# Low parts of the second recurrence's weight tiles: made by GpSimd instead of VectorE

## What is computed

```python
h = rms_norm_2(x, attn_norm)
z = h @ w_in                                   # 1024 pool, 3 x 1024 r/k/v, 288 low-rank columns
pool_out = einsum(causal_multiscale_pool(z_pool), pool_w) * pool_scale
rwkv_out = rwkv7_time_mix(...)                 # S = S*w + (S a) b' + v k', y = S r, 16 heads of 64
x = x + concat(pool_out, rwkv_out) @ w_out
x = x + square(relu(rms_norm_2(x) @ w_ffn_up)) @ w_ffn_down
x = x + sigmoid(rms_norm_2(x) @ w_ple_gate) * (p @ w_ple_proj)
```

## Time and profile before

| | |
|---|---|
| median of 3 runs | 2878.07 us (2876.27 to 2879.27) |
| the profiled execution, its own time | 2877.43 us |
| its span in the profile | 2875.6 us |
| PE busy | 2797.9 us, 97% of the span |
| DVE busy | 1897.8 us, 66% |
| ACT busy | 1493.3 us, 52% |
| POOL busy | 161.3 us, 6% |
| low parts on DVE | 901 instructions, 1119.4 us |

### The profile page before, as it was taken

One profiled execution on the slowest core, in us unless ns is written; L12 is line 12 of the kernel. 1 busy time (PEld: TensorE's weight loads), 2 busy tenths in 40 slices (PEclk: granted clock), 3 DMA queues, 4 the chain that ended last, 5 costly groups with the idle time before them and its releaser, 6 DMA issues.

```text
span 2875.6 us, 40645 instructions
## 1 busy us (share of the span) xinstructions
PE 2797.9 (97%) x16324; PEld 2445.5 (85%) x16324; DVE 1897.8 (66%) x2237; ACT 1493.3 (52%) x2026; POOL 161.3 (6%) x131
## 2 busy tenths in 40 slices
PE   8999999999999999999999998989999999999998
PEld 8988987888888888888888997877788888888886
DVE  6467765555668777777777676666666666666665
ACT  5346555544455545455546565545544444444464
POOL 1010111000000000000000022111000000000000
PEclk9999999999999999999999999999999999999999
DMA  6544443466666666666665532222555565555554
GB/s 221 186 154 145 153 123 114 136 196 187 184 195 185 194 191 195 190 189 187 190 192 177 187 125 69 94 74 92 177 190 191 186 196 192 187 196 191 192 169 161
DMA packets 133820, 485.47 MB, mean 169 GB/s; under 512 B 14944, under 2 KB 16352, under 8 KB 133120
## 3 DMA queue, kind: packets, MB, share of 16 engines
q1 hardware_dynamic: 133632, 482.87, 53.1%
HBM read 480.71 MB, written 2.10 MB: 168 GB/s over the span
## 4 chain that ended last, share of the span: by engine, by line
PE 84%; DVE 7%; ACT 4%; issue 3%; DMA 1%; POOL 0%; DVEq 0%; ACTq 0%; SPq 0%; POOLq 0%
PE psm L193 77%; PE psb L193 6%; ACT ar L209 2%; DVE ar L231 2%; DVE ar L221 1%; PE psb L196 1%; DMA raw<-in_w_in 1%; DVE slo L221 1%; ACT shi L209 1%; DVE x L221 1%; DVE gs L231 0%; DVE ar L235 0%; ACT L209 0%; DVE gf L221 0%; POOL ar L221 0%
## 5 line engine op out<-in xcount | busy, mean ns | idle before, releaser
L221 DVE TENSOR_TENSOR slo<-raw,shi 128x1024 fp32r<-128x1024 f32 (+1 forms) x901 | 1119.4, 1247 | 629.7 <-ACT shi L209 627.1
L209 ACT ACTIVATE shi<-raw 128x1024 fp32r<-128x1024 f32 (+1 forms) x901 | 945.8, 1053 | 1012.4 <-PE psm L193 811.6
L193 PE MATMUL psm<-shi,gs 128*128 128x512 f32 x2016 | 645.4, 394 | 0.8 <-ACT ar L209 0.8
L193 PE MATMUL psm<-hs,shi 128*128 128x512 f32 (+1 forms) x2528 | 564.1, 347 | 0.0
L193 PE MATMUL psm<-gs,shi 128*128 128x256 f32 (+2 forms) x2592 | 550.2, 330 | 12.5 <-DVE slo L221 11.9
L193 PEld LDWEIGHTS psm<-gs,shi 128*128 128x128 f32 (+1 forms) x2592 | 431.8, 191 | 51.3 <-DVE slo L221 12.5
L193 PEld LDWEIGHTS psm<-hs,shi 128*128 128x128 f32 x2528 | 427.5, 190 | 47.6 <-issue 0.6
L193 PE MATMUL psm<-shi,hs 128*128 128x512 f32 x1408 | 450.3, 393 | 3.9 <-DVE hs L221 2.9
L193 PEld LDWEIGHTS psm<-shi,gs 128*128 128x128 f32 x2016 | 380.3, 189 | 80.0 <-issue 1.6
L193 PE MATMUL psm<-slo,gs 128*128 128x512 f32 x1008 | 393.9, 391 | 0.0
L193 PE MATMUL psm<-gs,slo 128*128 128x256 f32 (+1 forms) x1808 | 366.5, 284 | 0.0
(11 more groups left out here) (185 smaller groups left out, 1712.2 us busy)
## 6 DMA issues: line engine op xcount, KB each, us to landing
raw<-in_w_in SPq DMA_DIRECT2D x240, 512.0 KB, 3.6
raw<-in_w_up SPq DMA_DIRECT2D x176, 512.0 KB, 4.2
raw<-in_w_ffn_up SPq DMA_DIRECT2D x128, 512.0 KB, 4.1
raw<-in_w_ffn_down SPq DMA_DIRECT2D x128, 512.0 KB, 3.3
raw<-in_w_down SPq DMA_DIRECT2D x88, 512.0 KB, 4.0
raw<-in_w_out SPq DMA_DIRECT2D x64, 512.0 KB, 3.9
raw<-in_w_ple_gate SPq DMA_DIRECT2D x32, 512.0 KB, 4.1
raw<-in_w_branch_b SPq DMA_DIRECT2D x16, 512.0 KB, 3.6
```

The lines of the kernel that those rows point to most:

```text
L193: return self.issued(self.eng and self.eng.matmul(out, lhs, rhs, start=start, stop=stop, skip_group_check=True), cost)
L209: return self.issued(self.eng and self.eng.activation(out, in_, fn, scale=scale, **kw), cost)
L221: return self.issued(self.eng and self.eng.tensor_tensor(out, a, b, op), self.cost(out))
```

## The change

GpSimd gets a program `lows` that makes the low parts of the tiles of `rkv`, `pool`, `out2a`, `out2b` and `pp` (100 tiles, all 128x1024) with a counter of its own, `lo_pool`; VectorE's `lows` passes over them. TensorE, SyncE and the planner ask for the counter that belongs to the tile. Everything else is as before, but the planner now sees a VectorE with less and a GpSimd with more to do, and writes another order for this part. In the diff the first `lows` is VectorE's, the second GpSimd's.

```diff
+        on_pool = set()
+        for name in plan:
+            if name[0][0] in ("rkv", "pool", "out2a", "out2b", "pp"):
+                on_pool |= set(range(end[name[0]] + 1 - len(name[1]), end[name[0]] + 1))
+
+        def low_done(j):
+            return lo_pool if j in on_pool else lo_done
...
-                        pe.wait_ge(hi_done if joined else lo_done, j)
+                        pe.wait_ge(hi_done if joined else low_done(j), j)
...
             def lows():
                 for j, (_, _, kc, _, n) in enumerate(tiles):
                     m = kc * n
+                    if j in on_pool:
+                        yield
+                        continue
                     v.wait_ge(hi_done, j)
...
+            def lows():
+                for j, (_, _, kc, _, n) in enumerate(tiles):
+                    m = kc * n
+                    if j in on_pool:
+                        p.wait_ge(hi_done, j)
+                        p.tt(slo[:, j % NS, 0:m], raw[:, j % NR, 0:m], shi[:, j % NS, 0:m].bitcast(F), ALU.subtract,
+                             turn=False).then_inc(lo_pool, j)
+                    yield
...
-                        sp.wait_ge(lo_done, j)
+                        sp.wait_ge(low_done(j), j)
                         bring(j + NR)
...
-                    at = lo_done.time(j)
+                    at = low_done(j).time(j)
```

More of the change, by code:

```diff
@@ L495, in build @@
         landed = [count(f"landed{i}", 16) for i in range(NR)]
-        hi_done, lo_done, tile_done = count("hi_done"), count("lo_done"), count("tile_done")
+        hi_done, lo_done, lo_pool, tile_done = [count(n) for n in ("hi_done", "lo_done", "lo_pool", "tile_done")]
         pe_step, act_step, dve_step, pool_step = [count(n + "_step") for n in ("pe", "act", "dve", "pool")]
@@ L501, in build @@
         stored = count("stored", 16)
-        counts = [*landed, hi_done, lo_done, tile_done, pe_step, act_step, dve_step, pool_step, *loaded.values(), stored]
+        counts = [*landed, hi_done, lo_done, lo_pool, tile_done, pe_step, act_step, dve_step, pool_step, *loaded.values(), stored]
         banks = Banks([psb[:, i, :] for i in range(4)])
@@ L730, in weights @@
                                     yield
-                            pe.wait_ge(lo_done, j)
+                            pe.wait_ge(low_done(j), j)
                             for q, f in blocks:
@@ L2487, in pair @@
                 yield from inverse(("pair", c), inv, G[:, :, 1, 0, :], (dve_step, ("G", c, 3)), None, masks)
-            progs = {"boot": boot(), "rope": rope(), "open_second": open_second()}
+            progs = {"boot": boot(), "rope": rope(), "open_second": open_second(), "lo": lows()}
             progs |= {("squares", 0, f): squares_in(f) for f in range(4)}
```

## The result

The changed kernel takes 2911.61 us (median of 4 runs, 2909.74 to 2914.32) against 2877.52 for the kernel before beside it; the ratio is 1.0118, 95% interval 1.0106 to 1.013. That is 34.1 us more. I had forecast 2878 with a range to 2899, so the time lies outside the range, on the side of the rival "the conflict wins", which I had priced at +14 (15.9 at most).

The account below looks back on a forecast made before the run. The prediction took TensorE, busy for 97% of the span, to bound the kernel. Its terms, -10.6 + 7.9 + 2.7, summed to 0.0 us against the profiled 2877.4 us, giving 2878 with a range of 2861 to 2899.

Parts of the forecast that it names:

- the conflict wins: Rival: in the dense stretches, waits of VectorE's bursts and GpSimd's steps exceed the 10.6 us relief; +14, 2892 us; chance 0.26.
- What bounds the kernel: Whole span: TensorE, busy for 97%; idle time and clock in the pairs' time leave 42 us at most to give back.
- The relief, -10.6: Nine places in the dense stretches where TensorE's chain sat out a VectorE low part; removing them gains 10.6 us.
- the fifteen places: Places between 1646 and 2027 us where the chain sat out a low part; together 17.4 us, the bound if all count.
- The conflict, +7.9: Dense stretches: VectorE's bursts reading two SBUF operands wait for GpSimd low parts; 7.9 us, bounds nothing and twice that.
- GpSimd's chain steps, +2.7: Dense stretches: some 13 chain visits to GpSimd wait 0.42 us each behind low parts, 5.4 us; half reaches TensorE.
- A burst that meets one: Dense stretches: a VectorE burst meeting a GpSimd low part waits half of 2.41 us; 19 x 0.35 x 1.2 = 7.9 us.
- the two dense stretches: 1750 to 1800 and 1850 to 1960 us, where TensorE's idle time sits, 9.9 and 13.4 us, with few weight tiles to fill in.
- 19 in the 160 us of both dense stretches: Count of VectorE bursts that can meet a low part, taken from four in the 34 us from 1761 to 1795.
- GpSimd's pace, taken as zero: Tiles ahead of the first pair and behind the last: GpSimd's 2.5 us per tile keeps up; zero cost, bound 31.7 us.
- The order, taken as nothing: Planner ends the last pair's chain about eight tiles earlier, leaving less tile work to hide a late step; no cost priced.
- the signs I had listed: Trace signs to tell cases apart: TensorE's busy and idle time, POOL's `slo` length and waits, growth of VectorE's two-SBUF forms.

Follow-up runs that it names:

- the first experiment: All queues in the order of the kernel before, the 100 low parts moved to GpSimd only after planning; 2892.48 us, ratio 1.0058 to the kernel before.
- experiment 27: Not a run: the text reads "in the first experiment", then a count, 27 of the 50 held steps; the run is the first experiment.
- The outer tiles alone: The changed kernel's queues, GpSimd making only the first 27 and last 24 low parts, VectorE the 49 between; 2896.25 us, ratio 1.0067 to the kernel before.
- the run with the relief alone: Order of the kernel before, GpSimd making each of 100 low parts by two zero fills that read nothing; 2861.62 us, ratio 0.995 to the kernel before.

## Why the prediction was wrong

**What bounds the kernel.** Right. TensorE does, and the change gave and took only in its idle time and clock between 1560 and 2060.

**The relief, -10.6.** The mechanism was right. The size was -15.4 in the order of before, inside my bound of 17.4, but with fills of 1.9 us for a tile; with a GpSimd as slow as in the change it is about 11 by the estimate above, so that it was sized too low is not shown. The make-up was wrong: I had left the clock out of the term, and 6 of the 15 us are busy time. Which of the fifteen places counted was not measured.

**The conflict, +7.9, and GpSimd's chain steps, +2.7.** This is the step that failed most: 30.5 us in the old order, 33.8 in each of two others, against 10.6; without the 4 us of length still some 26 and 29.6. Three of its terms were too small.
- "A burst that meets one waits half of 2.41 us in the mean." I had 19 x 0.35 = 6.7 such waits of 1.2 us. In the first experiment, with the queues in the order that I had read, 23 of VectorE's steps in the two dense stretches take over 0.3 us longer than the shortest of their form, by 1.05 us in the mean; in the kernel before 9 do, by 0.42. So the single wait was about right and their number was not. The two-element operations ahead of the pairs wait 2.2 us each, one after the other: a burst can lose the way at each of its steps, so long as GpSimd has another low part ready, and low parts come in runs.
- "An operation of VectorE that reads two operands from SBUF stands still". Those with one tensor operand do too: `x<-x,gf` went from 484 to 1526 ns and a copy of two elements to 5.98 us in one run. These I had not counted. With a GpSimd that only writes, the two-input steps were nearly free (485 and 534 ns) and `x<-x,gf` still took 920 ns.
- "19 in the 160 us of both dense stretches". The time outside of these was taken at nothing, for both the steps there and the tiles ahead of the first pair. The outer tiles alone cost 8.9 us, and in the first experiment 27 of the 50 steps that were held stand outside.

The Trainium skill has the second of these. "SBUF — State Buffer", section "Who interferes with whom", says that copies and `tensor_scalar` can run in a mode that takes the shared ports and then contend with any GpSimd instruction, while a two-input `tensor_tensor` contends only with one that reads. By that rule, the traces agree: 920 ns under fills for the scaling, 485 for `ar<-ar,par`. I had cited the section for the second half only. It says that whoever issues first has the ports for its whole instruction; in the run with pieces of 512 columns one blocked VectorE copy also missed four starts of GpSimd's next piece.

**GpSimd's pace, taken as zero.** Right in its own terms: 2.42 us, and with fills as long as that, but without reads, TensorE is busy for 89.69 us from 1560 to 1650. The sentence that "VectorE has little left there that could disturb" looked at the wrong direction. It is VectorE that is disturbed, and through it ScalarE's high parts.

**The order, taken as nothing.** Wrong: +10.4 alone, +19.0 on top of the moved work. "It leaves less tile work to hide a late step" had no price, and nothing in the trace of before gives one. Whether it is the cause was not shown.

**The rivals.** The conflict rival named the right cause and most of the place; its upper end of 15.9 was built from the same bursts and half waits. Of the signs I had listed, these were right: `slo` at 2.4 us, the growth of `ar<-ar` and `ar<-ar,par` with `ar<-psb,con` unchanged, idle time over 38 (51.0 of the 350 us from 1650 to 2000, against 28.2). These were wrong: TensorE full from 1600 to 1650 (it was busy for 47.9), and no wait for POOL's `slo` over 1 us (2.1).

## What to carry to other kernels

Before work goes to GpSimd, count the instructions that VectorE begins while GpSimd will be running, one by one, copies and scalings with them, and price each at up to a whole GpSimd operation; size does not protect a small one. What GpSimd saves VectorE must be more than that: here 124 us of work moved away, 11 to 15 us of it on the path, and 26 to 34 us came back, by whether GpSimd's own length is counted to the first or to the second. And where a planner writes the queues, price the new plan as a change of its own by building both halves: the old order with the new engine, the new order with the old engine.

## What was not expected of the hardware

VectorE steps with two inputs of two elements per partition take as long as GpSimd's 1024-column operation when they meet one (2.3 us against 0.16). A reciprocal and a reduction of that size, beside the same run of low parts, took 0.17 and 0.16 us. GpSimd's operations in a row kept VectorE out over several of them once: 5.98 us for a copy, with pieces of 1.25 us, where no other step was held for more than 1.1. Steps of VectorE that read PSUM were not slowed at all (424 ns in both kernels). A fill of 1024 columns on GpSimd takes 0.96 us, a subtraction of the same width 2.42. The granted clock can add to what idle time costs, at no fixed rate: in the run with the relief alone 9.2 us less idle time came with 6.1 us less busy time for the same matmuls (clock of 0.98 against 0.96 from 1650 to 2000), with the first 27 tiles on GpSimd 4.3 us more idle time with 0.2 us less.
